# Redistributing modulation blocks over three stages and reordering stage ends in a two-part transformer-like kernel

## The reference

```python
def modulate(x, g, shift, scale):
    return rmsnorm(x, g) * (1 + scale) + shift
...
def first_block(x, c, ctx, c_ctx, mod_w, mod_b, ...):
    # each of two layers: six vectors of 1024 (shift, scale, gate, twice) = silu(c) @ mod_w[l] + mod_b[l],
    # once for the 256 latent tokens and once for the 256 context tokens
    # x = x + gate * mixer(modulate(x, ...)); x = x + gate * ffn(modulate(x, ...))
...
def second_block(x, ...):
    # w_in product (85 x 128 columns), four branches, x + merged @ w_out
```

## Time and profile before

| what | value |
|---|---|
| median of three runs | 1832.86 us (1831.72 to 1836.36) |
| the profiled execution's own time | 1833.69 us |
| its span | 1832.0 us |
| TensorE busy | 1717.1 us, 94% of the span |
| VectorE busy | 1347.4 us, 74% |
| ScalarE busy | 848.5 us, 46% |
| mean granted clock of TensorE | 0.978 |
| moved by DMA | 237.45 MB, mean 130 GB/s |

### The profile page before, as it was taken

The page is one execution under the profiler, slowest core; times in us unless marked ns, Lnnn a source line. Parts: engine busy times, 40 slices in busy tenths (PEclk is TensorE's granted clock), DMA queues, the critical chain, the costliest instruction groups (busy, mean ns, idle before and its releaser), DMA issues. The chain is left out here.

```text
span 1832.0 us, 26450 instructions
## 1 busy us (share of the span) xinstructions
PE 1717.1 (94%) x10228; PEld 1463.3 (80%) x10228; DVE 1347.4 (74%) x2522; ACT 848.5 (46%) x1476; POOL 55.3 (3%) x113
## 2 busy tenths in 40 slices
PE   4899999798999999999899898999998999999997
PEld 3788877576888888877688776988898988999997
DVE  6677883865999999958995477479875445765594
ACT  2623344635544443245454465433344467665541
POOL 0900000000000000000000000000000000000000
PEclk9999999999999999999999899999999999999999
DMA  8343341031332226724563101444555454444442
GB/s 320 109 156 110 125 131 54 1 121 63 102 103 95 92 92 214 232 94 157 176 201 122 58 1 40 146 152 154 154 183 185 137 176 134 143 129 127 150 157 86
DMA packets 65462, 237.45 MB, mean 130 GB/s; under 512 B 7423, under 2 KB 8888, under 8 KB 65080
## 3 DMA queue, kind: packets, MB, share of 16 engines
q1 hardware_dynamic: 63416, 233.13, 39.3%
q10 hardware_dynamic: 1920, 2.63, 0.5%
HBM read 234.41 MB, written 1.05 MB: 129 GB/s over the span
## 5 line engine op out<-in xcount | busy, mean ns | idle before, releaser
L458 PE MATMUL banks<-m,weights_high 128*128 128x256 f32 (+1 forms) x4336 | 1046.9, 334 | 45.4 <-DVE weights_low L494 33.6
L458 PEld LDWEIGHTS banks<-m,weights_high 128*128 128x128 f32 x4336 | 738.2, 192 | 139.2 <-issue 31.8
L458 PE MATMUL banks<-m,weights_low 128*128 128x256 f32 (+1 forms) x2168 | 715.8, 330 | 0.0
L494 DVE TENSOR_TENSOR weights_low<-weight_ring,weights_high 128x1024 fp32r<-128x1024 f32 x293 | 355.9, 1223 | 239.4 <-ACT weights_high L489 238.6
L458 PEld LDWEIGHTS banks<-m,weights_low 128*128 128x128 f32 x2168 | 415.5, 192 | 38.1
L489 ACT ACTIVATE weights_high<-weight_ring 128x1024 fp32r<-128x1024 f32 x293 | 309.2, 1057 | 262.3 <-PE banks L458 217.1
L626 DVE SCALAR_TENSOR_TENSOR m<-m,columns 128x189 f32<-128x189 f32 (+4 forms) x856 | 321.9, 452 | 19.3 <-ACT m L566 19.2
L765 DVE SCALAR_TENSOR_TENSOR m<-weight_ring,m 128x1024 bf16<-128x1024 f32 x184 | 225.1, 1223 | 17.7 <-DMA weight_ring<-in_weights 11.9
L565 ACT ACTIVATE m<-banks,columns 128x512 f32<-128x512 f32 (+1 forms) x120 | 83.2, 694 | 299.1 <-PE banks L458 298.9
L458 PE MATMUL banks<-m,weight_ring 128*128 128x256 f32 x704 | 152.1, 379 | 0.0
L458 PEld LDWEIGHTS banks<-m,weight_ring 128*128 128x128 f32 x704 | 133.7, 190 | 18.1
(11 more groups left out here) (383 smaller groups left out, 1637.2 us busy)
## 6 DMA issues: line engine op xcount, KB each, us to landing
weight_ring<-in_weights SPq DMA_DIRECT2D x433, 512.0 KB, 3.7
x<-in_tokens SPq DMA_DIRECT2D x1, 2048.0 KB, 14.1
m<-in_cmp_w SPq DMA_DIRECT2D x1, 2048.0 KB, 7.4
m<-in_cond SPq DMA_DIRECT2D x2, 512.0 KB, 4.9
out<-x ACTq DMA_DIRECT2D x8, 128.0 KB, 1.9
columns<-in_columns SPq DMA_DIRECT2D x1, 633.0 KB
m<-in_rg_w ACTq DMA_DIRECT2D x1, 512.0 KB, 3.5
m<-in_spatial_w ACTq DMA_DIRECT2D x1, 512.0 KB
```

What stands on the lines that cost most here:

```text
L458: mm = pe.matmul(out, lhsT, rhs, start=p.start and i == 0, stop=p.stop and i == len(passes) - 1)
L494: dve.tensor_tensor(w_lo[:, g % PARTS, :], K.ring[:, PLACE[PRODUCT_BLOCKS[g]] % RING, :], w_hi[:, g % PARTS, :].bitcast(F32), ALU.subtract ...
```

## The change

It has six parts. (1) mod1's blocks are laid over three stages: 27 in down0, 15 in ssd_in, 6 in ssd_out; the last six (gate of the feed-forward) are used in down1 only. (2) `own`: in a stage whose last item is a residual tile, the last tile is added, squared and only then the next stage's blocks are split. (3) In `Normalise.scalar` the high part of feature 0 follows its own affine step; those of features 1 and on stand where they stood. (4) In even_in ScalarE's table is loaded one tick earlier and its three wide operations come one tick later. (5) 13 filler matmuls at ssd_in's end, 8 at in2's. (6) 8 at merge's start.

```diff
--- before.py
+++ after.py
@@ -100,7 +100,8 @@
 MOD_PE = 4
 SQUARES_AT = 2
 MOD_EVEN = 44
-MOD_DOWN = 24
+MOD_DOWN = 27
+MOD_ODD = 42
 DOWN_FIRST = 4
 DOWN_TOGETHER = 2
 MOD_SSD = 25
@@ -110,9 +111,10 @@
     + blocks_of("even_out")[:TOGETHER] + spread_among(blocks_of("mod0")[MOD_EVEN:], blocks_of("even_out")[TOGETHER:]) \
     + blocks_of("up0") + blocks_of("down0")[:DOWN_FIRST] \
     + spread_among(blocks_of("mod1")[:MOD_DOWN], blocks_of("down0")[DOWN_FIRST:]) \
-    + blocks_of("ssd_in")[:TOGETHER] + spread_among(blocks_of("mod1")[MOD_DOWN:], blocks_of("ssd_in")[TOGETHER:MOD_SSD]) \
+    + blocks_of("ssd_in")[:TOGETHER] + spread_among(blocks_of("mod1")[MOD_DOWN:MOD_ODD], blocks_of("ssd_in")[TOGETHER:MOD_SSD]) \
     + blocks_of("ssd_in")[MOD_SSD:]
-for _name in ("ssd_out", "up1", "down1", "in2", "branch2", "out2"):
+STREAM += spread_among(blocks_of("mod1")[MOD_ODD:], blocks_of("ssd_out"))
+for _name in ("up1", "down1", "in2", "branch2", "out2"):
     STREAM += blocks_of(_name)
 PLACE = {b: i for i, b in enumerate(STREAM)}
 assert sorted(STREAM) == list(range(N_BLOCKS))
@@ -398,6 +400,9 @@
         return max(begun, min(n_known, sum(p <= PLACE[b] + PARTS for p in places)))
     due = np.maximum.accumulate([parts_due(first + b) for b in last_of]).tolist()
     due[-1] = n_known
+    own = list(due)
+    if items[-1].on == "dve" and first + last_of[-1] in PART:
+        own[-1] = PART[first + last_of[-1]] + 1
     ahead = parts_due(first + last_of[convs[-1]]) + AHEAD if convs and convs[-1] + 1 < len(items) else 0
     if prepare:
         prepare.take([a[:, i, :] for a, m in ((acc, ACC), (raw, RAW)) for i in range(m)] if convs else None)
@@ -529,7 +534,7 @@
                     while n_cast < n_conv:
                         cast_high(n_cast)
                         n_cast += 1
-                while n_high < due[e]:
+                while n_high < own[e]:
                     high_part(act, n_high)
                     n_high += 1
                 if not it.conv and n_finish < n_conv:
@@ -539,6 +544,9 @@
                 if it.on != "act":
                     beside.scalar(act, e, free_dve.at(rank[e]))
                     beside.half("scalar", act, 2 * e + 1)
+                    while n_high < due[e]:
+                        high_part(act, n_high)
+                        n_high += 1
                     continue
                 if ended[e] < 0:
                     beside.half("scalar", act, 2 * e + 1)
@@ -652,7 +660,7 @@
 
                 if it.on == "dve":
                     flush()
-                low_parts(due[e])
+                low_parts(own[e])
                 beside.half("vector", dve, 2 * e)
                 if it.on == "dve":
                     dve.wait_ge(K.done.sem, done0 + e + 1)
@@ -666,6 +674,7 @@
                         group = []
                 beside.vector(dve, e, free_act.at(rank[e]))
                 beside.half("vector", dve, 2 * e + 1)
+                low_parts(due[e])
             flush()
             if mods:
                 while mod_places:
@@ -894,8 +903,8 @@
                 ins.then_inc(*self.ready.up())
                 continue
             ins.then_inc(*self.whole.up())
-            if k:
-                high_part(k - 1)
+            if k != 1:
+                high_part(max(k - 1, 0))
         if self.plain is None:
             high_part(KD - 1)
 
@@ -1531,8 +1540,9 @@
         K, f, B = self.K, self.f, self.BANK
         link = Link(act, self.scalar_step)
         e = self.e
-        yield self.DECAYS
+        yield self.DECAYS - 1
         act.preload_act_table_set(LOG_EXP)
+        yield self.DECAYS + 1
         act.wait_ge(*self.z_read.at(1))
         act.activation(e, self.banks(), ACT.Abs).then_inc(*self.absed.up())
         act.wait_ge(*self.absed.at(1))
@@ -2024,19 +2034,22 @@
 
 def odd_mixer(K, mods):
 
+    modulator, blocks = mods
+    late = MOD_ODD - MOD_DOWN
     with K.scope():
         zs, xl, xc = K.take(KI, LAT), K.take(KI, LAT), K.take(KI, CTX)
         bt, ct, dcol = K.take(SG, T), K.take(SG, LAT), K.take(4, 64)
         rows = K.take(LAT, dtype=F32R), K.take(LAT, dtype=F32R)
         state = xc.rearrange("p (g i) t -> p g (i t)", g=SG).rearrange("p g (d x) -> p g d x", d=2)
         with K.activations(KD * T):
-            ssd_projection(K, zs, xl, xc, bt, ct, dcol, rows, state, mods)
+            ssd_projection(K, zs, xl, xc, bt, ct, dcol, rows, state, (modulator, blocks[:late]))
         with K.scope():
             normed = ssd_latent(K, xl, zs, bt, ct, dcol, rows, state)
         with K.activations(KI * LAT):
             parts = Split(K, [(xl[:, c, :], *K.h_parts(LAT, c)) for c in range(KI)], normed)
             run_products(K, residual_items(K, "ssd_out", KI, lambda k: K.h_parts(LAT, k), CTX,
-                                           lambda m, which: K.mod[:, 1, 16 + m, which:which + 1]), prepare=parts,
+                                           lambda m, which: K.mod[:, 1, 16 + m, which:which + 1]),
+                         (modulator, blocks[late:]), prepare=parts,
                          beside=SumSquares(K, CTX), banks=BANKS - 1, fill=8)
 
 
@@ -2064,7 +2077,7 @@
                             lambda act, bank, c=c: act.activation(zs[:, c, :], bank[:, 0:LAT], ACT.Silu))])
         tile += KD
     run_products(K, first_together(rounds), mods, prepare=Normalise(K, 0, "mix_g1", (1, 0, 8)), beside=steps, banks=4,
-                 acc_slots=SSD_ACC, fill=16)
+                 acc_slots=SSD_ACC, fill=16, tail=13)
 
 
 SSD_ACC = 6
@@ -2528,7 +2541,7 @@
     rstd = K.take(LAT)
     spare = [f[name][:, j, :] for name in ("ga", "gb", "gc") for j in range(KB)]
     run_products(K, first_together(rounds), prepare=NormaliseTwice(K, CTX, "final_g", "norm2", spare, rstd),
-                 beside=HybridSteps(K, f, item_of, rstd), banks=3, fill=8)
+                 beside=HybridSteps(K, f, item_of, rstd), banks=3, fill=8, tail=8)
 
 
 class Scratch:
@@ -3245,7 +3258,7 @@
         for it in last[0]:
             it.made = lambda k: 4 * k + 3
         store = Store(K, out, len(rounds))
-        run_products(K, rounds + last, prepare=parts, beside=store)
+        run_products(K, rounds + last, prepare=parts, beside=store, fill=8)
     with nc.Block() as block:
         @block.sync
         def _(sync):
```

## The result

The changed kernel takes **1821.66 us** (median of 4 runs, 1820.83 to 1825.16) against 1834.61 for the kernel before on the same chip (1831.72 to 1837.02): ratio 0.9928, 95% interval 0.991 to 0.9946. The forecast was 1820, range 1814 to 1827, and faster by over 0.3% with a chance of 0.87. Its profiled execution took 1821.29 us with a span of 1819.6, against 1833.69 and 1832.0: 12.4 less, where the sum of the prediction said 13.2. The forecast stood on a kernel before of 1832.86; beside the changed kernel it took 1834.61, a difference as large as the 1.7 us by which the median missed 1820.

A forecast was written before the change was run, and what follows sets the result against it. TensorE was taken as the bound almost everywhere, VectorE in the first two thirds of ssd_in. The terms summed to -13.2 us against the profiled 1833.69, so 1820.5, put at 1820 for the runs' median of 1832.86; range 1814 to 1827.

The forecast's parts named there:

- Modulation blocks: Moving nine out of ssd_in, three to down0 and six to ssd_out: 12.2 us saved in ssd_in, 0.3 lost in ssd_out.
- b7, b13 and b24: Weight blocks of ssd_in: TensorE's stops ahead of them go, saving 4.0, 6.4 and 2.3 us with slow clock and restart.
- b11: Weight block of ssd_in: a stop of about 2.2 us stays, 0.3 saved; the slow clock may or may not follow.
- b23: Weight block of ssd_in: its low part waits behind conv taps and one modulation block; 2 us stop left, 0.1 saved.
- down0's reserve: down0: three more modulation blocks cost 0, since low parts stay early; least spare 2.7 us, at block 5.
- ssd_out: Six modulation blocks over 16 low parts: two places cost 0.15 us each, 0.3 slower.
- rival for slower: ssd_out: loads run behind, each of six modulation blocks costs 2.5 plus 1.8 us, 26 in all: 1846; chance 0.04.
- Tile first: Last residual tile before the splits at stage ends: 0.5 us slower at down0, 1.0 at down1, 0 at even_out.
- a rival at 2 x 1.8: Later barriers' idle time slows products behind them, fillers' worse ends hold, 2 us more at late low parts: 1829; chance 0.09.
- First feature: Its high part comes earlier at stage starts: 0.55 us saved in up0, 0.6 in ssd_in, 0 in even_in.
- Bank in even_in: TensorE's 4.10 us wait for a bank ScalarE must read moves up by one reading: 0.5 us saved, not 4.
- Fillers: ssd_latent: first slow-clock stretch sped up, second untouched, 0.85 us net saved with the later barrier; merge: 0.3 saved.

The follow-up runs named there:

- The undoing: The changed kernel with its modulation blocks back where they were (24 in down0, 24 in ssd_in, none in ssd_out): 1831.83 us, ratio 0.998.
- the tile back: The changed kernel with the residual tile behind the next stage's splits again: 1818.63 us, ratio 0.9908.
- the fastest version: The changed kernel with the residual tile behind the splits, 21 modulation blocks over ssd_in's b3 to b36, none in ssd_out: 1809.21 us; run again, 1808.53, ratio 0.9869.

## Why the prediction was right

- **Modulation blocks** (-12.2, +0.3). Right in size by two ways: alone they give 11.9 us, and in the changed kernel's profile b7, b13 and b24 don't stop, b11 stops for 1.91 (2.2), b23 for 2.33 (2.0). The undoing gave 9.9, on intervals of 2.4 each. Subtracting the removed blocks from the times of the low parts was enough. At b11 the clock stayed up and at b23 it fell (0.83 over 940 to 950), the reverse of what I weighed, at the same price; with the blocks alone, and with the tile back, it fell behind both.
- **down0's reserve** (0). Right: no stop with 27, four small ones with 30.
- **ssd_out** (+0.3). Right: 0.3 by the table. Its rival for slower (0.04) is real, but begins at nine blocks.
- **Tile first** (+0.5, +1.0, 0). The sign was right, and so were the barriers against the one profile of before: 0.5, 1.2, 0. By the runs without it the edit costs 2.4 to 3.7 us by the ratios and 3.1 to 3.9 by the stage ends, not 1.5. **This is the term that was mis-sized**, for two reasons. The 6.0 us of the earlier trace rows held slow sums of squares (1.89 us where they else take 1.13), so the barrier at down0's end costs 1.3 and not 0.5 against an undisturbed one. And the sum left out the slower fillers behind it, part of what I had put into a rival at 2 x 1.8: the 16 of ssd_in take 3.81 us where the clock stays up and 5.44 to 6.17 behind an idle 3.79 us.
- **First feature** (-0.55, -0.6). Where the clock is up it is 0.84 in each of the two stages: from the stage's start to the first product 5.52 us in the kernel before with MOD_SSD = 33, 4.68 in the fastest version. In the changed kernel the slow fillers behind the tile-first barrier hide most of it at ssd_in: 5.19.
- **Bank in even_in** (-0.5). The wait fell from 4.10 to 3.6, as forecast; even_in and even_out together didn't get shorter (380.0 before, 380.3 and 380.0 after). Over all fourteen profiles they take 377.2 to 382.7 us, with and without the edit, so 0.5 can't be seen there.
- **Fillers** (-0.85, -0.3). At ssd_latent -2.8 in the pair of profiles, within the bounds given, and about -2.5 in the mean of all fourteen. The first slow stretch is gone in all ten profiles with the fillers (1.00 over the first 4 us behind the first matmul, against 0.50 to 0.69 without). I had argued that the second one follows on thin work of TensorE that fillers don't touch. That holds in part: a slow stretch that begins 4 to 7 us behind the first matmul is left in eight of the ten, 3 to 8 us long, and in two, of the kernel with 21 blocks over b3 to b36, there is none. The section "HAM oscillation" of the Trainium skill, "TensorE: Matmul & The Clock Gate", which ties the lower level to idle time of TensorE, agrees with the first stretch (TensorE idle for 4.04 us ahead of it without the fillers, for 1.52 with them) and with the fillers at the two ends above. In merge they are worth 0.3 in the mean of the profiles, the -0.3 of the sum. The times put the three fillers together at 0.6 to 1.1 us, not resolved.

The misses cancelled: about 2 us less from the tile, about 2 us more from the fillers. The times fit this: from the blocks alone (0.9935) to all but the tile first (0.9908), the other small edits are worth 5.0 us, where the sum had 2.8, with an uncertainty of some 3 us. That the gain came so near to the forecast is in part luck.

## What to carry to other kernels

To see whether work can be moved off an engine that bounds a stage, list the times at which its critical operations run, subtract what stood ahead of them, and compare with the time at which the consumer asks: here this gave 11.9 us, where the runs gave 11.9 and, by undoing, 9.9; and the place inside the stage was worth as much attention as the stage. An edit that starts the last result sooner is no gain where the barrier waits for something else; look at what now ends last, and at how long TensorE idles ahead of it, since the work behind can be slower for it. And look whether the profile of before that prices the edit was itself disturbed at that place. Before a stage's difference of 1 to 3 us is explained, profile the unedited kernel twice.

## What the runs showed of the hardware

- Behind a stage end with TensorE's idle time in short pieces the fillers ran faster than behind one long piece. At down0's end, with the tile behind the splits, pauses of 0.87, 1.06 and 0.30 us between sums of squares (2.23 in all) were followed by the 16 fillers in 3.81 us in six of nine profiles, and in 4.46 to 4.75 in three; with the tile first, one pause of 3.79 us was followed by 5.44 us in three and 6.15 or 6.17 in two of five. At down1's end the 8 fillers took 2.02 us in eight and 2.65 in one, and behind one pause of 3.66 us 3.14 to 3.75 in five. Here length and shape of the idle time changed together, and no run tells them apart. The products that follow are no such clean case: their clock fell in six of nine and in three of five.
- The clock can fall without a difference in the program: the kernel before took 1.89 us for the last sums of down0, and its barrier came 6.0 us after TensorE was done; with another number for ssd_in, which nothing up to there depends on, the same sums took 1.13 us and the barrier 5.2.
- One and the same stop can leave the clock up or bring it down: behind the stop of 2.6 to 3.1 us at down1's start the granted clock over 10 us was 0.69 to 0.70 in three, 0.83 to 0.86 in six and 1.00 in five of fourteen profiles, worth some 3 us between the ends.
